# Gate projections of a hybrid encoder layer moved behind the attention heads, twelve of sixteen panels as 2x2 blocks

## The reference

```python
u = rmsnorm(h, norm_g[l, 0])
proj = u @ w_in                      # 1024 x 1024 by 1024 x 5120
hc, bc, cc, q, k, v, gates = jnp.split(proj, offs, axis=-1)   # 512 each, gates 2048
inner = cc * hc                      # conv over three tokens, then y_conv = (bc * conv) @ w_conv_out
# per head (4 heads): two score maps with ALiBi bias, softmax each, a = softmax(s1) - lam * softmax(s2)
o = a @ v;  o = rmsnorm(o, subln_g) * (1 - lam_init);  y_attn = o @ w_attn_out
g = sigmoid(gates + b_gate)
merged = g[:, :, 0] * y_conv + g[:, :, 1] * y_attn
m = merged @ w_o;  h = h + rmsnorm(m)
f = square(relu(rmsnorm(h) @ w_ff1)) @ w_ff2;  h = h + rmsnorm(f)
```

## Time and profile before

| | |
|---|---|
| median of three executions | 1436.82 us (1436.71 to 1437.62) |
| the profiled execution | 1436.46 us, its span 1434.7 us |
| PE matmul busy | 1394.5 us, 97% of the span |
| DVE busy | 924.4 us, 64% |
| ACT busy | 567.0 us, 40% |
| mean granted PE clock | 0.994 of full speed |

### The profile page before, as it was taken

The page is one execution under the profiler, slowest core; times in us unless marked ns, Lnnn a source line. Parts: engine busy times, 40 slices in busy tenths (PEclk is TensorE's granted clock), DMA queues, the critical chain, the costliest instruction groups (busy, mean ns, idle before and its releaser), DMA issues.

```text
span 1434.7 us, 17064 instructions
## 1 busy us (share of the span) xinstructions
PE 1394.5 (97%) x6281; PEld 1131.5 (79%) x6281; DVE 924.4 (64%) x1306; ACT 567.0 (40%) x871; POOL 111.3 (8%) x73
## 2 busy tenths in 40 slices
PE   5999999999999999999999999999999999999997
PEld 4877778777787777878788877888888877888886
DVE  6485576757657664156555698667774677775576
ACT  5434443533434454211233344333332444454453
POOL 0000000000000000000000143323333100000000
PEclk9999999999999999999999999999999999999999
DMA  5211111111111112344542155444444955336333
GB/s 166 59 30 59 42 33 60 44 29 44 58 29 29 58 66 74 103 154 143 192 165 72 44 169 161 143 152 161 161 147 148 387 199 170 102 97 226 95 111 132
DMA packets 141463, 161.96 MB, mean 113 GB/s; under 512 B 6813, under 2 KB 88922, under 8 KB 141274
## 3 DMA queue, kind: packets, MB, share of 16 engines
q1 hardware_dynamic: 135392, 148.40, 32.1%
q10 hardware_dynamic: 6010, 12.75, 2.3%
HBM read 114.98 MB, written 46.14 MB: 112 GB/s over the span
## 4 chain that ended last, share of the span: by engine, by line
PE 76%; DVE 10%; ACT 5%; issue 5%; DMA 4%; SPq 0%; ACTq 0%; DVEq 0%
PE psum L711 40%; PE psum L890 17%; PE psum L951 12%; DMA f_raw<-f_scratch 3%; PE psum L781 2%; PE psum L766 1%; PE psum L879 1%; DVE op L1749 1%; DVE v L1769 1%; PE psum L770 1%; DVE t_sum L1665 1%; DVE op L1752 1%; DVE v L1876 1%; ACT op L1253 1%; ACT w_hi L993 1%
## 5 line engine op out<-in xcount | busy, mean ns | idle before, releaser
L951 PE MATMUL psum<-op 128*128 128x512 f32 x1344 | 307.7, 390 | 2.9 <-DVE op L1752 2.6
L951 PEld LDWEIGHTS psum<-op 128*128 128x128 f32 x1344 | 251.4, 188 | 59.0 <-issue 4.4
L711 PE MATMUL psum<-act_hi,w_hi 128*128 128x512 f32 x640 | 257.8, 403 | 2.6 <-ACT staging L1059 2.3
L711 PE MATMUL psum<-act_hi,w_lo 128*128 128x512 f32 x640 | 250.4, 391 | 0.0
L711 PE MATMUL psum<-act_lo,w_hi 128*128 128x512 f32 x640 | 250.0, 391 | 0.0
L711 PEld LDWEIGHTS psum<-act_hi,w_hi 128*128 128x128 f32 x640 | 120.6, 188 | 31.7 <-issue 8.3
L711 PEld LDWEIGHTS psum<-act_hi,w_lo 128*128 128x128 f32 x640 | 120.5, 188 | 25.8
L711 PEld LDWEIGHTS psum<-act_lo,w_hi 128*128 128x128 f32 x640 | 120.8, 189 | 25.4 <-issue 1.9
L1749 DVE TENSOR_TENSOR op<-v,op 128x512 fp32r<-128x512 f32 x112 | 78.3, 699 | 71.1 <-ACT op L1253 71.1
L1396 DVE TENSOR_TENSOR w_lo<-w_raw,w_hi 128x1024 fp32r<-128x1024 f32 x52 | 65.1, 1252 | 82.0 <-ACT w_hi L993 80.2
L1253 ACT ACTIVATE op<-v 128x512 fp32r<-128x512 f32 x112 | 70.4, 628 | 118.2 <-DVE v L1769 69.1
(11 more groups left out here) (218 smaller groups left out, 2470.2 us busy)
## 6 DMA issues: line engine op xcount, KB each, us to landing
f_raw<-f_scratch SPq DMA_DIRECT2D x112, 256.0 KB, 2.7
w_raw<-in_w_in SPq DMA_DIRECT2D x40, 512.0 KB
w_raw<-in_w_ff SPq DMA_DIRECT2D x32, 512.0 KB, 4.9
f_scratch<-f_out SPq DMA_DIRECT2D x56, 256.0 KB, 2.3
gates_scratch<-staging ACTq DMA_DIRECT2D x32, 256.0 KB, 2.0
gate_in<-gates_scratch SPq DMA_DIRECT2D x16, 512.0 KB, 4.2
v<-in_w_ff SPq DMA_DIRECT2D x8, 1024.0 KB, 7.9
v<-in_w_ff SPq DMA_DIRECT2D x4, 2048.0 KB, 10.4
```

The costliest lines, as they stand in the source:

```text
L711: mm = nc.tensor.matmul(bank, stat(a, kt), moving(b, kt), start=(n == 0), stop=(n == len(terms) - 1))
L951: mm = nc.tensor.matmul(psum[:, (X_BANK, Z_BANK)[m % 2][t]], op[n % SLOTS][:, 2 + a, token_cols(t)], op[n % SLOTS][:, b], start=(m in (0, ...
```

## The change

The turn of a head loses its four gate units, and its other entries are put in a new order: v0 and v1 stand behind S0 and S1, `VT` behind h0, one unit stands between each two score blocks, and the three taps of the convolution become an entry of their own, `K`, before b0. vt, which was held in one of the map buffers, now lies in `staging`. All 16 gate panels come after the heads. Four of them (eight units) are made as before, in one turn with the end of the last head, each in a PSUM bank of its own where there is one. The other twelve are made as six pairs by the block scheme of FF1, on which both stages now share the classes and helpers `Pairs`, `pair_order` and `pair_term`. For the gate pairs each weight block has one set of buffers, DVE makes the token sums (`t_sum`, 10 instructions, and 4 `t_lo`), and z and o are split at the end of the last pair, their low parts in the place of z and o themselves.

```diff
-TURN = steps("C7 q0 O0 q1 T7 TL7 k0 AV1 k1 v0 O1 v1 S0 VT0 h0 X0 M0 C0 h1 S1 X1 T0 M1 TL0 C1 c0 S2 X2 T1 M2 "
-             "TL1 C2 c1 S3 X3 b0 T2 M3 TL2 C3 b1 S4 X4 g0 T3 M4 TL3 C4 g1 AV0 S5 X5 T4 M5 TL4 C5 g2 S6 X6 T5 "
-             "M6 TL5 C6 g3 S7 X7 T6 M7 TL6")
+TURN = steps("C7 q0 O0 q1 T7 TL7 k0 AV1 k1 O1 S0 X0 v0 M0 C0 S1 X1 T0 M1 TL0 C1 v1 S2 X2 T1 M2 TL1 C2 h0 VT0 S3 X3 T2 M3 TL2 "
+             "C3 h1 S4 X4 T3 M4 TL3 C4 c0 AV0 S5 X5 T4 M5 TL4 C5 c1 S6 X6 T5 M6 TL5 C6 K0 b0 S7 X7 T6 M7 TL6 b1")
-AFTER = [steps("C7 g0 O0 g1 T7 TL7 ZS0 g2 AV1 ZS1 g3 O1 ZS2"), steps("ZS3 OS0 g0 OS1 g1 OS2 g2 OS3 g3")]
+AFTER = steps("C7 g0 O0 g1 T7 TL7 g2 AV1 g3 g5 O1 g4 g7 g6")
+GATE_BANKS = (0, 1, 2, 3, 4, 5, 0, 1)
+GATE = Pairs(GATE_PANELS // 2, KT - GATE_PANELS // 2, ("X2", "Z1", "Y", "X3", "X4", "Z2"), (0, 0))
...
+            for p in range(GATE.first, GATE.end):
+                if p == GATE.first:
+                    sp.wait_ge(w_split, P_BR)
+                elif p == GATE.first + 1:
+                    sp.wait_ge(t_split, GATE.t_split_at(1))
+                else:
+                    sp.wait_ge(g_split, PART_AT["W22", p - 2])
+                pair_load(GATE, w_in_t, p, COL_G // P + 2 * p)
...
-            wait(act, a_ready, i * QB)
+            if not (isinstance(i, int) and i == 0):
+                act.wait_ge(tb_done, tb_use(i - 1, "VT", 0) + 1)
             nc.scalar.activation(vt[:, half_cols[h]], psum[:, h], ACT.Copy).then_inc(vt_ready, 1)
...
+            def x_copy(st, k, p):
+                n = st.n(p)
+                act.wait_ge(mix_done, st.at(f"X{k}", p))
+                if st is FF1:
+                    act.wait_ge((f11_sum, f21_sum, f22_sum)[k - 1], n)
+                elif p > st.first:
+                    act.wait_ge(gate_ready, GATE_AT[((2 * p - 2, 0), (2 * p - 1, 0), (2 * p - 1, 1))[k - 1]])
+                nc.scalar.activation(st.sums[k - 1][:], psum[:, st.slot(p)], ACT.Copy)
...
+            for p in range(GATE.first, GATE.end - 1):        # ACT's part of a pair
+                if p > GATE.first:
+                    g_part_hi("S1", p)
+                    gate_block("C22", p - 1)
+                x_copy(GATE, 1, p)
+                g_part_hi("W11", p + 1)
+                if p > GATE.first:
+                    gate_block("C12", p - 1)
+                g_part_hi("S4", p)
+                gate_block("C11", p)
+                g_part_hi("W12", p + 1)
+                if p > GATE.first:
+                    gate_block("C21", p - 1)
+                g_part_hi("W22", p)
+                x_copy(GATE, 2, p)
+                g_part_hi("S2", p + 1)
+                g_part_hi("S3", p + 1)
+                x_copy(GATE, 3, p)
```

More of the change, by code:

```diff
@@ L800, in _, with mix @@
                 walk(i, TURN)
-            walk(HEADS, AFTER[0], True)
-            walk(HEADS + 1, AFTER[1], True)
-            pe.wait_ge(s_read, HEADS * QB)
+            walk(HEADS, AFTER, True)
+            def mix(bank, stat, moving, first, last):
+                terms = [(kt, a, b) for kt in range(KH) for a, b in PASSES]
+                for n, (kt, a, b) in enumerate(terms):
+                    mm = nc.tensor.matmul(bank, stat[a][:, kt], moving(b)[:, kt], start=(first and n == 0),
+                                          stop=(last and n == len(terms) - 1), skip_group_check=True)
+                mm.then_inc(mix_done, 1)
@@ new lines, in _ @@
+            p = GATE.end - 1
+            g_part_hi("S1", p)
+            gate_block("C22", p - 1)
+            x_copy(GATE, 1, p)
+            gate_block("C12", p - 1)
+            g_part_hi("S4", p)
+            gate_block("C21", p - 1)
+            g_part_hi("W22", p)
+            x_copy(GATE, 2, p)
+            last_turn("ZS0 ZS1 ZS2 ZS3")
+            act.wait_ge(mix_done, GATE.at("Z1", p))
+            last_turn("OS0 OS1")
+            gate_block("C11", p)
+            x_copy(GATE, 3, p)
@@ L1566, in _, with last_turn @@
                 walk(i, TURN)
[L1567 to L1570 removed]
+            def last_turn(text):
+                walk(HEADS, steps(text), True)
+            p = GATE.first
+            last_turn("C7")
+            for k in range(3):
+                t_sum(GATE, 1, k)
+            last_turn("O0 TL7 g1")
@@ new lines, in _ @@
+            t_lo(GATE, 1)
+            g_sum("S4", p)
+            t_sum(GATE, 4, 1)
+            t_lo(GATE, 4)
+            for p in range(GATE.first, GATE.end - 1):
+                if p > GATE.first:
+                    gate_sum("C22", p - 1)
+                    g_part_lo("S1", p)
+                g_sum("S3", p + 1)
+                g_sum("S1", p + 1)
+                g_part_lo("W11", p + 1)
+                g_part_lo("S4", p)
+                gate_sum("C11", p)
+                if p == GATE.first:
+                    last_turn("O1")
+                g_part_lo("W12", p + 1)
+                g_sum("S2", p + 1)
+                g_sum("S4", p + 1)
+                if p > GATE.first:
+                    gate_sum("C21", p - 1)
+                g_part_lo("W22", p)
+                g_part_lo("S2", p + 1)
+                g_part_lo("S3", p + 1)
@@ new lines, in _ @@
+            p = GATE.end - 1
+            gate_sum("C22", p - 1)
+            for x in ("S1", "S4"):
+                g_part_lo(x, p)
+            gate_sum("C21", p - 1)
+            g_part_lo("W22", p)
+            last_turn("ZS0 ZS1 ZS2 ZS3")
+            gate_sum("C11", p)
+            last_turn("OS0 OS1")
+            split_lo(P_BR, P_BR % RING)
+            gate_sum("C22", p)
+            last_turn("OS2 OS3")
+            gate_sum("C21", p)
+            split_lo(P_BR + 1, (P_BR + 1) % RING)
```

659 lines of the change are left out of this document (408 added, 251 removed).

## The result

The changed kernel takes **1455.45 us** (median of four, 1452.54 to 1457.15), beside 1436.82 before: slower, by a ratio of 1.0126 (95% interval 1.0107 to 1.0145). Forecast were 1465 and a range of 1453 to 1477. The profiled execution took 1454.18 us, 17.7 more than the profiled one of before, where the sum had said 28.3. So direction and places were right, and 10.6 us of cost too many were counted. The time lies in the stated range near its lower end, and outside the narrower one that the forecast itself was given (1459 to 1471).

What follows compares the result with a forecast made beforehand. PE, busy 97% of the span, was taken to set the time. Terms -16.4, -4.9, +33.7, +6.8, +0.6 and +8.5 sum to +28.3 on 1436.5, with 0.4 for the median 1465 us; range 1453 to 1477, own range 1459 to 1471.

Steps and rivals of the forecast that it cites:

- 72 matmuls: Gate panels: 576 matmuls become 504, 72 fewer at 0.228 us each, -16.4 us.
- waits on gates, their clock: PE's 3.3 us of waits on gate units' banks and 1.6 us of clock behind one go: -4.9 us.
- start of each head: New waits before S0, S1 and T0: 8.5 us in head 1, 8.4 in each of three others, +33.7 us.
- clock behind T0: Half clock behind the gap before T0, paid in full in each head: 4 x 1.7, +6.8 us.
- rest of a turn: Later blocks of each head: T2 waits 0.75 us, T6 0.2; before's 1.8 and 1.4 taken out: +0.6 us.
- gate stage: After the heads, +8.5 us: AV1 1.5, X2 1.4, X3 2.7 plus 1.7 clock, last pair's X3, X4, Z2 1.2.
- The stated bound of error: Turn of a head: the prediction called itself wrong if it got over 16 us shorter; it expected 12.
- the gaps leave the clock alone: Rival: new PE gaps behind DVE and ACT don't lower the clock; about 1456 us, chance 0.14.
- X2 of the first pair: Gate stage: ACT's high part of T4 stands before its first copy out of the X bank; 1.4 us.
- pairs starve: Rival, gate stage: each of the four middle pairs waits 2 us, with some clock; 1475 us, chance 0.18.
- heads stay hidden: Rival of the other sign: heads lose nothing, sum -12.8, 1424 us; chance 0.05.

Runs made afterwards that it cites:

- v0_mended: Changed kernel with v0 ahead of S0, v1 behind C0, VT and taps moved, table scaled before k1's low part; 1426.02 and 1426.65 us, ratios to before 0.9939 and 0.9930.
- filled: Changed kernel with unused matmuls in PE's gaps, 12 ahead of S0 and 10 ahead of T0; 1451.79 us, ratio to before 1.0113.
- mended_all: v0_mended with copy2's edit and, on DVE in the last turn, O0 and TL7 ahead of the first token sums; 1430.67 us, ratio to before 0.9964.
- copy2: Changed kernel with the first gate pair's second copy out of the X bank moved ahead of C11 on ACT; 1457.20 us, ratio to before 1.0154.

## Why the prediction was right where it was, and wrong where it was

Losses below are measured on PE from start to start, less the work between, in the profile of the changed kernel.

| term | forecast | measured | |
|---|---|---|---|
| 72 matmuls | -16.4 | -16.4 | count as said |
| waits on gates, their clock | -4.9 | -5.2 | gone |
| start of each head | +33.7 | +31.4 | S0 13.6, S1 4.2, T0 10.9, v0 at half clock in heads 1 and 2 2.7 |
| clock behind T0 | +6.8 | +3.2 | in two heads of four |
| rest of a turn | +0.6 | +0.9 | by the waits: T2 0.8, T6 0.2 a head, less 3.2 of before |
| gate stage | +8.5 | +5.8 | AV1 1.0, X3 2.3 + 1.6 clock, last pair 0.9 |
| w_o's first gap | 0 | -1.7 | same gap of 2.0 us, clock up this time |
| sum | +28.3 | +18.0 | 17.7 by the two profiles |

**The start of a head** was right in mechanism and nearly in size. Counted as the forecast counts, from the start of k1's copies (270.88 in head 3), S0 starts at 3.9, S1 at 13.1 and T0 at 17.4 us, where 3.8, 13.1 and 17.5 were said. A head without a fall of the clock loses 3.2, 1.8 and 2.7 us for a forecast of 3.6, 2.1 and 2.6. The 0.4 us less at S0 are a misreading: O1 was taken for 0.45 us of PE's work, from its start to the next unit's, but that unit's first matmul then holds PE for 0.4 us more, in both kernels. Before, head 4, timeline of PE:

```profile
423.14 1.02 PE L793 MATMUL psum<-dev,ones 128*128 128x512 f32 x2
423.60 0.80 PE L711 MATMUL psum<-act_hi,w_hi 128*128 128x512 f32 x1
424.24 0.40 PE L711 MATMUL psum<-act_lo,w_hi 128*128 128x512 f32 x1
```

What makes the three waits was shown by moving one at a time: a unit in front of S0 ends S0's wait, O1 (with O0 and AV1) and the table moved away end S1's, and the copy moved as well ends T0's. v0_mended, with a unit in front, v1 behind C0, M0 ahead of it and the table early, comes out as worked out from these rows. The stated bound of error, a turn over 16 us shorter, wasn't reached (14.2).

**The clock** is the step that failed: "The one before T0 is paid in full: 4 x 1.7", 6.8 us, of which 3.2 came. It rested on three cases, all of which had fallen. Heads 3 and 4 of the same profile refute it, and with it that the gap before S0 always lowers the clock: it did so in heads 1 and 2 only. Windows of 1 us of PE in the changed kernel (length, busy, granted clock, DMA share, GB/s), behind T0 of head 2 and of head 3:

```profile
178.00:179.00 1.00, 1.00 (x7) 0.50 0.00 0
179.00:180.00 1.00, 1.00 (x5) 0.50 0.00 0
...
289.00:290.00 1.00, 1.00 (x8) 1.00 0.00 0
290.00:291.00 1.00, 1.00 (x6) 1.00 0.00 0
```

Both gaps are 2.5 us behind the same DVE instruction. The rival "the gaps leave the clock alone", 1456, came nearest in number, but its mechanism is no truer: half of the falls came, and `filled` speaks for it that they followed idle time, for with PE at work in these gaps its profile has none in the heads. What I should have put in was a chance for each gap, not a certainty.

The Trainium skill's page "TensorE: Matmul & The Clock Gate", section "Why this matters for your kernels", has a loop in which DVE copies out of PSUM, the next matmuls follow at once and the clock stays up. The prediction read from it that gaps behind DVE and ACT cost only themselves, but in that loop PE has no gap, so it says nothing of one. Here such a gap did lower the clock: the 3.91 us one behind DVE's k_lo in head 1 is followed by half clock. Between 40 and 1120 us no gap of 0.6 us or more in any of the runs ended with a DMA.

**The gate stage** was 2.7 us too dear. X2 of the first pair started 0.1 us behind the end of its copy and without a wait, where 1.4 us were said. mended_all, whose PE arrives earlier, shows that the margin was that thin. AV1 (1.0 for 1.5), X3 (2.3 for 2.7) and the last pair (0.9 for 1.2) are a little under what was worked out. The middle pairs take 19.04 to 19.11 us from X1 to X1 with PE never idle, so the rival "pairs starve" is out. That w_o's gap came without its clock was nobody's doing: it is the chance named above, on the other side.

**The rival of the other sign** ("heads stay hidden") failed as said, at S0. But v0_mended shows that it needed only another order.

## What to carry to other kernels

When a change takes filler work out of a hand-written order, ask which gaps that filler covered and where the remaining pieces must stand. The order alone was worth 29 us here, nearly twice the 16.4 us of matmuls that the change saved. A unit brings more than its matmuls: v1 carried a weight split, and where it stood between X0 and M0 it made S1 wait 4 us. Two waits in series hide each other, so remove them together before you judge either; and where PE waits for a chain on other engines, moving one piece of it can just move the wait to the next consumer (copy2, mended_all).

## What the runs showed of the hardware

For all PE gaps of 0.6 us or more between 40 and 1120 us in the thirteen profiles, I took from windows of the trace whether the granted clock went from full to half within about 2 us of the gap's end, before or behind it (lengths rounded to 0.1 us):

| idle time ahead | clock fell |
|---|---|
| 3.9 us and more | 28 of 28 |
| 2.4 to 3.1 | 20 of 34 |
| 2.0 to 2.3 | 11 of 30 |
| 1.5 to 1.9 | 1 of 14 |
| under 1.5 | 0 of 115 (3 more lay in a stretch already at half) |

No fall in this part of the program came without such a gap. Identical gaps differ from one profile to the next: w_o's of 2.01 us was followed by half clock in five of thirteen. A stretch at half clock was mostly 3.4 us, sometimes 6.8, twice 10.2. Its price ran up to half its length but was often less, since a slower PE waits less at its next wait: the changed kernel's turn from head 2 had 6.7 us at half clock and was 1.6 us longer than the one from head 3, with S1's wait down from 1.65 to 0.29 us. What decides between two gaps of one length these traces don't say. Nor is it shown that such falls make the spread of the changed kernel's runs (4.6 us): only one of them has a trace, and the mean granted clocks (0.991, 0.990, 0.992 and 0.989 for 1452.54, 1454.18, 1456.73 and 1457.15 us) don't follow the times.
